# A recurrence's diagonal, moved behind the first level's product and made with a matrix of ones

## What is computed

```
for each of 4 heads (q, k, f, v are 1024 tokens x 128):
    S_t = diag(f_t) S_{t-1} + k_t v_t^T        # k = 1 - f
    o_t = S_t^T q_t
```

## Time and profile before

| What | Value |
|---|---|
| time, median of 3 runs | 1888.99 us (1888.77 to 1889.04) |
| time of the profiled execution | 1889.1 us |
| its span | 1887.5 us |
| PE busy | 1869.3 us (99%) |
| DVE busy | 1126.6 us (60%) |
| ACT busy | 676.1 us (36%) |
| POOL busy | 406.1 us (22%) |
| granted TensorE clock | 1.00 |

### The profile page before, as it was taken

How to read it: one execution, slowest core, us unless ns; L and a number is a source line. 1 busy time by engine, 2 the same in 40 slices (tenths; PEclk the granted TensorE clock), 3 DMA queues, 4 the chain that set the end, 5 groups by cost and what they waited for, 6 DMA issues and landing times. The chain is left out here.

```text
span 1887.5 us, 24459 instructions
## 1 busy us (share of the span) xinstructions
PE 1869.3 (99%) x9171; PEld 1545.9 (82%) x9171; DVE 1126.6 (60%) x1591; ACT 676.1 (36%) x1029; POOL 406.1 (22%) x319
## 2 busy tenths in 40 slices
PE   9999999999999999999999999999999999999999
PEld 8888888888888888888888667888888888888887
DVE  6966666665556641156667773377666656655464
ACT  7423323233334533210223663353323333333332
POOL 2043422341103110002222310000434222411030
PEclk9999999999999999999999999999999999999999
DMA  5355444437866433324343410133554454368653
GB/s 182 112 201 184 145 169 161 161 129 253 312 198 191 133 129 122 138 90 139 133 139 111 150 60 1 68 112 112 195 184 151 155 174 148 142 238 309 219 193 139
DMA packets 221341, 296.52 MB, mean 157 GB/s; under 512 B 15377, under 2 KB 117913, under 8 KB 221234
## 3 DMA queue, kind: packets, MB, share of 16 engines
q1 hardware_dynamic: 206752, 262.19, 40.8%
q0 software_dynamic: 6272, 18.14, 2.9%
q10 hardware_dynamic: 8210, 14.75, 2.0%
HBM read 206.13 MB, written 92.56 MB: 158 GB/s over the span
## 5 line engine op out<-in xcount | busy, mean ns | idle before, releaser
L710 PE MATMUL ps<-hThi,whi 128*128 128x512 f32 x888 | 346.6, 390 | 0.2 <-DVE hid L1735 0.2
L712 PE MATMUL ps<-hThi,wlo 128*128 128x512 f32 x888 | 345.6, 389 | 0.0
L711 PE MATMUL ps<-hTlo,whi 128*128 128x512 f32 x888 | 345.6, 389 | 0.0
L710 PE MATMUL ps<-whi 128*128 128x512 f32 x616 | 240.0, 390 | 0.0
L712 PE MATMUL ps<-whi,wlo 128*128 128x512 f32 x616 | 239.7, 389 | 0.0
L711 PE MATMUL ps<-wlo,whi 128*128 128x512 f32 x616 | 239.7, 389 | 0.0
L710 PEld LDWEIGHTS ps<-hThi,whi 128*128 128x128 f32 x888 | 166.7, 188 | 35.1 <-issue 0.9
L712 PEld LDWEIGHTS ps<-hThi,wlo 128*128 128x128 f32 x888 | 166.7, 188 | 34.7
L711 PEld LDWEIGHTS ps<-hTlo,whi 128*128 128x128 f32 x888 | 166.7, 188 | 34.1
L710 PE MATMUL ps<-hXhi,whi 128*128 128x512 f32 x480 | 186.9, 389 | 0.7 <-issue 0.7
L712 PE MATMUL ps<-hXhi,wlo 128*128 128x512 f32 x480 | 186.8, 389 | 0.0
(11 more groups left out here) (218 smaller groups left out, 2827.9 us busy)
## 6 DMA issues: line engine op xcount, KB each, us to landing
hid_scratch<-hid SPq DMA_DIRECT2D x132, 256.0 KB, 3.3
raw<-ffn_w_gate SPq DMA_DIRECT2D x44, 512.0 KB, 3.7
raw<-ffn_w_up SPq DMA_DIRECT2D x44, 512.0 KB, 4.9
wdb<-ffn_w_down SPq DMA_DIRECT2D x44, 512.0 KB, 4.1
wd_scratch<-wdb SPq DMA_DIRECT2D x88, 256.0 KB, 4.3
raw<-hid_scratch SPq DMA_DIRECT2D x80, 256.0 KB, 2.7
rawx<-hid_scratch SPq DMA_DIRECT2D x74, 256.0 KB, 2.8
raw<-w_in SPq DMA_DIRECT2D x28, 512.0 KB, 5.0
```

The source lines that it names most:

```text
L710: pe.matmul(dst, ahi, bhi, start=first, stop=False, skip_group_check=onto)
L711: pe.matmul(dst, ahi, blo, start=False, stop=False, skip_group_check=onto)
L712: return pe.matmul(dst, alo, bhi, start=False, stop=last, skip_group_check=onto)
```

## The change

The diagonal's product changes its place and its kind. Before, PE made it at place 2 from `hK` and `fQ`, as eight float32 matmuls, and level 1 followed at place 3. Now level 1 stands at place 2 and the diagonal at place 4. DVE multiplies keys and queries elementwise into `aT` (two halves), ACT copies that to float32r (`diag_high`), DVE makes the low part (`diag_low`), and PE multiplies a 128x128 matrix of ones by both: four matmuls of 512 columns in float32r, which sum over the features. What PE leaves is kept as before, times the identity, but now behind step L = 2 of DVE's chain, right ahead of the keeping of level 1. ACT waits for the elementwise product ahead of its first tile of the group. At the beginning the low part of the first weight stands one place earlier in DVE's list, and two idle products of six are left out. The `ones` are made once, and three semaphores are merged into one, without other effect on order.

```diff
-LEVEL_AT = {2: 0, 3: 1, 5: 2, 6: 3, 8: 4, 9: 5, 10: 6, 12: 7}
+LEVEL_AT = {2: 1, 4: 0, 5: 2, 6: 3, 8: 4, 9: 5, 10: 6, 12: 7}
...
-            idle_products(6)
+            idle_products(4)
...
-                        pe.wait_ge(scaled, 9 * j + L + 1)
+                        pe.wait_ge(scaled, 9 * j + (2, 1, 3, 4, 5, 6, 7, 8)[L])
                         if L == 0:
 
                             pe.wait_ge(ro_ready, j + 1)
-                            for c in range(TT):
-                                mm = pe.matmul(ps[:, c * P:(c + 1) * P], hK[:, c * P:(c + 1) * P],
-                                               fQ[:, c * P:(c + 1) * P], start=True, stop=True)
+
+                            for h in range(2):
+                                at = slice(h * HALF, (h + 1) * HALF)
+                                pe.matmul(bank(h), ones[:, :], diag_high[:, at], start=True, stop=False)
+                                mm = pe.matmul(bank(h), ones[:, :], diag_low[:, at], start=False, stop=True)
...
             def group(n0, advn, func, feature=False, head=None, first_head=False, square_at=()):
+                if head is not None:
+                    act.wait_ge(diag_made, head + 1)
+                    act.activation(diag_high[:, :], aT[:, :], ACT.Copy).then_inc(diag_hi, 1)
                 for o in range(7):
...
             early_lo_part(1, 0)
+            weight_lo(0, 0)
             early_lo_part(2, 0)
-            weight_lo(0, 0)
             early_lo_part(3, 0)
...
                 dve.wait_ge(read_done, j + 1)
                 link(dve.tensor_tensor(hQ[:, :], fQ[:, :], fF[:, :], ALU.mult))
                 pair_keys(1)
-                dve.wait_ge(scaled, 9 * j + 1)
                 dve.nop().then_inc(scaled, 1)
-                keep_scores(0)
+
+                q = fQ[:, :].rearrange("p (a par t) -> p a par t", par=2, t=P)
+                kq = aT[:, :].rearrange("p (a par t) -> p a par t", par=2, t=P)
+                link(dve.tensor_tensor(kq[:, :, 0, :], k[:, :, 0, :], q[:, :, 0, :], ALU.mult))
+                dve.tensor_tensor(kq[:, :, 1, :], k[:, :, 1, ::-1], q[:, :, 1, :], ALU.mult).then_inc(diag_made, 1)
+                dve.wait_ge(diag_hi, j + 1)
+                dve.tensor_tensor(diag_low[:, :], aT[:, :], diag_high[:, :].bitcast(F32), ALU.subtract).then_inc(scaled, 1)
...
-                    dve.wait_ge(scores_done, 8 * j + L)
+                    dve.wait_ge(scores_done, 8 * j + (L if L > 2 else 1))
...
+                    if L == 2:
+                        keep_scores(0)
                     keep_scores(L - 1)
```

More of the change, by code:

```diff
@@ L319, in build @@
             mk = keep("mk", [P, (LEVELS - 1) * HALF], U8, c, "right")
+            ones = keep("ones", [P, P], F32R, c, "right")
             sso = keep("sso", [P, TT], where=c, side="right")
             rso = keep("rso", [P, TT], where=c, side="right")
+        with ExitStack() as c:
+            keep("clear_of_fF_to_tot", [P, 7 * T], where=c, side="right")
+            diag_low = keep("diag_low", [P, T], F32R, c, "right")
+            keep("clear_of_kS", [P, T], where=c, side="right")
+            diag_high = keep("diag_high", [P, T], F32R, c, "right")
         with ExitStack() as c:
@@ L430, in build @@
         proj_stored = [sem(f"proj_stored{s}") for s in range(2)]
-        lb_diff = sem("lb_diff")
-        lb_sig = sem("lb_sig")
-        lb_ready = sem("lb_ready")
+        lb_step = sem("lb_step")
         sig_ready = sem("sig_ready")
@@ L484, in build @@
         cat_loaded = sem("cat_loaded")
+        diag_made = sem("diag_made")
+        diag_hi = sem("diag_hi")
         pool_passed = sem("pool_passed")
@@ L974, in _ @@
             group(2, 0, False, nothing)
+            pe.wait_ge(mask_set, LEVELS)
             pe.nop().then_inc(k_turned, 1)
@@ L1483, in _ @@
             group(0, 0, ACT.Silu, True)
-            act.wait_ge(lb_diff, 1)
-            act.activation(lb[:, 0, :], lb[:, 2, :], ACT.Sigmoid).then_inc(lb_sig, 1)
-            act.wait_ge(lb_ready, 1)
+            act.wait_ge(lb_step, 1)
+            act.activation(lb[:, 0, :], lb[:, 2, :], ACT.Sigmoid).then_inc(lb_step, 1)
+            act.wait_ge(lb_step, 3)
             group(1, 0, ACT.Sigmoid, True)
@@ L1927, in _ @@
             dve.wait_ge(lb_loaded, 16)
-            dve.tensor_tensor(lb[:, 2, :], lbs[:, 0, :], lbs[:, 1, :], ALU.subtract).then_inc(lb_diff, 1)
+            dve.tensor_tensor(lb[:, 2, :], lbs[:, 0, :], lbs[:, 1, :], ALU.subtract).then_inc(lb_step, 1)
             dve.wait_ge(setup_moved, 16)
@@ L1934, in _ @@
                    .then_inc(mask_set, 1)
+            dve.tensor_scalar(ones[:, :], ident[:, :], 0.0, 1.0, ALU.mult, ALU.add).then_inc(mask_set, 1)
             dve.wait_ge(rel_loaded, 16)
@@ L1946, in _ @@
                 split(P_MIX + 4 + q)
-            dve.wait_ge(lb_sig, 1)
-            dve.tensor_scalar(lb[:, 1, :], lb[:, 0, :], -1.0, 1.0, ALU.mult, ALU.add).then_inc(lb_ready, 1)
+            dve.wait_ge(lb_step, 2)
+            dve.tensor_scalar(lb[:, 1, :], lb[:, 0, :], -1.0, 1.0, ALU.mult, ALU.add).then_inc(lb_step, 1)
             for n in (1, 2):
@@ L1972, in keep_scores @@
                         dve.wait_ge(mask_set, LEVELS - 1)
-                    dve.wait_ge(scores_done, 8 * j + L + 1)
+                    dve.wait_ge(scores_done, 8 * j + max(L, 1) + 1)
                     if L == 0:
@@ L1996, in head @@
                 link(dve.tensor_scalar(k[:, :, 0, :], f[:, :, 0, :], -1.0, 1.0, ALU.mult, ALU.add))
-                dve.tensor_scalar(k[:, :, 1, :], f[:, :, 1, ::-1], -1.0, 1.0, ALU.mult, ALU.add).then_inc(scaled, 1)
+                link(dve.tensor_scalar(k[:, :, 1, :], f[:, :, 1, ::-1], -1.0, 1.0, ALU.mult, ALU.add))
                 dve.wait_ge(read_done, j + 1)
@@ L2058, in read_out @@
                    .then_inc(ro_ready, 1)
-            per_head = 5 + 5 * 7 + 2 * 6
+            per_head = 7 + 5 * 7 + 2 * 6
             dve.wait_ge(ext_stored, 16)
```

## The result

The changed kernel takes 1894.28 us (median of 11 runs, 1892.29 to 1895.06), the kernel before 1888.83 (11 runs, 1888.29 to 1889.38). The ratio is 1.0028, 95% interval 1.0020 to 1.0035: 5.4 us slower, 0.3%. The forecast was 1892.6 with a range of 1886.0 to 1894.2; the median lies 0.1 us above the range. The profiled execution took 1894.2 us, with a span of 1892.7, 5.2 more than before.

A forecast was written before the change was run, and what follows sets the result against it. PE, busy 99% of the span, was taken as the bound, with DVE's chain to level 3 just fitting. Head 0 -0.88, heads 1 and 2 +1.7 each, head 3 +1.1, beginning -0.05: +3.6, forecast 1892.6 us, range 1886.0 to 1894.2.

The forecast's parts named there:

- Direction and mechanism: Whole kernel 3.6 us slower: POOL's products hold DVE operations with two SBUF inputs, delaying level 3, despite PE's shorter list.
- What PE saves: Diagonal's product on PE: 0.91 us in float32r for 1.79 in float32, saving 0.88 a head, 3.5 in four.
- Place 2: Heads 1 to 3: level 1 waits 0.3 to 0.5 us for DVE's `hQ` and gathered keys; none in head 0.
- the 0.44: Lateness in us charged to level 1's start at place 2: 859.93 against PE's arrival at 859.49.
- Heads 1 and 2: Each 1.7 us longer, saving included: POOL holds DVE's low part and `hK`, and PE stands 2.2 us at place 6.
- the forecast's sequence on DVE: Heads 1 and 2: second product ahead of POOL, low part held by POOL's first product, `hK` by its second, level 3 late.
- rival C: Low part loses to both POOL products: 2.1 us for each of heads 1 and 2, +4.4 in all, 1893.4; chance 0.20.
- second way: POOL starts before DVE's second product, so ACT's copy is late too; priced the same, 2.1 us a head.
- Head 3: 1.1 us longer: low part free, POOL catches `hK`'s second half and the copies, level 3 at 992.4 against 991.34.
- so the delay stops there: After level 3: level 4 has 6.4 us of PE before it against some 4.3 on DVE, so no further delay.
- The beginning: First product some 0.4 us earlier, but ACT's bank emptying before the product at 28.73 leaves at most some 0.05 us.
- The chances: Odds for the whole change: slower 0.35, same 0.56, faster 0.09, with about 0.2% (3.8 us) distinguishable from no change.

The follow-up runs named there:

- e12: Changed kernel with POOL's two products of each head left out: 1886.30 us, ratio 0.9985 to the kernel before.
- e13: Kernel before with POOL's two products of each head left out: 1887.69 us, ratio 0.9992.
- e10: Changed kernel with eight small idle products on PE at place 6 of the last head alone: 1892.34 us, ratio 1.0017 to the kernel before.
- e9: Changed kernel with level 1's product at place 3 instead of 2, diagonal still at 4: 1892.93 us, ratio 1.0022 to the kernel before.
- e3: Changed kernel with POOL's two products of each head moved out of the stretch between level 1 and level 3: 1889.77 us, ratio 1.0003 to the kernel before.
- e6: Changed kernel without the diagonal's low part (DVE's subtraction and two of four float32r matmuls): 1889.21 us, ratio 1.0000 to the kernel before.

## Why the prediction was right and wrong

- **Direction and mechanism** were right: PE's list got shorter, and the ports shared by DVE and POOL took back more. e12 and e13 show it: +5.4 us with POOL's products, -1.4 without.
- **What PE saves**, 0.88 a head, is near what head 0 shows, 0.8 up to PE's arrival at place 2 of head 1; e12 is consistent with it once place 2 is charged in full.
- **Place 2**: waits of 0.43, 0.45 and 0.39 us, as forecast, but each costs a head about 0.67: the mis-sized term here is the 0.44, too small by 0.2. The 0.43 is idle time behind the record of the last matmul; from start to start level 1 is 859.38 - 858.79 = 0.59 late, and behind the wait it costs 0.1 more than the 0.9 of a level.
- **Heads 1 and 2**, forecast 1.7 each: 1.5 and 1.8 between starts at place 2. Head 2 followed the forecast's sequence on DVE to within 0.2 us at every step, up to level 3 at 16.35 us behind PE's arrival at place 2 (forecast 16.3). Head 1 followed rival C's second way (POOL ahead of DVE's second product, and place 4 waits 0.39). It was not dearer for it, since POOL was through when `hK` began: rival C's price for that way was wrong. That 1.5 lies near 1.7 is luck: it is made of waits of 0.43, 0.39 and 0.68 us, not of one of 2.2.
- **Head 3**, forecast 1.1: level 3's wait rose from 0.61 to 2.12 us, and relative to PE's arrival at place 2 level 3 came 1.0 us later (994.98 - 977.98 against 991.34 - 975.36). That is the size worked out, though POOL held both halves of `hK` and let the copies go, where the forecast had it hold the second half and the copies. What failed is the sentence on heads 1 and 2 that the sum for head 3 leans on, "so the delay stops there": I took a wait to cost its own length. Behind 2.1 us of standing still the granted clock fell, and that cost 1.6 us more; e10 takes it away by filling the wait and lands at 1892.34, and the two executions without the fall are 1892.29 and 1892.85, where the forecast had 1892.6.
- **The beginning**, forecast 0.05 us at most: 0.02 at the product named. By the start of the recurrence the changed kernel is 0.1 us late; that is not explained.
- **The chances**: "slower" had 0.35, less than "same". With the clock's 1.6 us in the sum it would have been the likeliest.

Open: why a wait of 2.17 us in e9 lets the clock fall and one of 2.33 in the same execution, like the 2.38 in e3, doesn't; and what decides in which executions of one kernel it falls.

## What to carry to other kernels

Where one engine is busy for 99%, look for the tightest handoff in the chain that feeds it and ask what a change puts ahead of that: two cheap operations moved into it cost 3.9 us here (3.0 without the fall of the clock), where the shorter products could save 3.5. Ahead of adding elementwise work on DVE, look up what POOL does at that moment, and which operands lie in SBUF. To a wait of PE of 2 us or more add 1.6 us in the price, since the clock may go with it. And where times of one kernel lie in two groups, look at the mean granted clock of each execution first: 0.999 against 1.000 told the groups apart in the changed kernel, e3, e6 and e9.

## What the runs showed of the hardware

- A wait of PE of 1.96 to 2.28 us was followed, in some executions and not in others, by some 3.4 us at the lower of the two clocks, which costs about 1.6 us (8.05 us for 6.45). Eight small matmuls on the identity in the wait kept the mean granted clock at 1.000 in all sixteen executions. Waits of 1.76 us and less in the recurrence, and two of 2.33 and 2.38, left it up in the profiled executions.
- A DVE operation with two SBUF inputs that starts behind a POOL product runs when that one ends, and then takes nearly its own length: one of 0.43 us (half of `hK`) ends 0.28 behind POOL (987.42 against 987.14), one of 0.69 ends 0.54 behind (862.95 against 862.41), one of 1.22 ends 1.09 behind (866.30 against 865.21). Copies from SBUF to SBUF are held too (two took 5.08 us for 0.62 in e6); operations with one input in PSUM kept their 0.69 and 2.27. POOL is held in the same way: 2.39 became 2.95 and 3.19 in head 2.
